# Index branch and S5 work moved between projection tiles, heads taken in pairs, and layer 0's S5 output table made by VectorE

## The reference

```python
for layer in range(DEPTH):                       # DEPTH = 2
    h = rms_norm(x, ln1_g[layer])
    (a_q, a_ckv, a_kr, i_q, i_k, i_w, b_u, c_q, c_kv, c_gate) = jnp.split(h @ w_in[layer], offsets, axis=-1)
    a_out = dsa_mixer(...)    # 4 heads; an indexer picks the 64 best keys of each query; latent keys and values
    b_out = s5_mixer(...)     # 16 groups of 16 channels, 64 complex states each, a linear scan over positions
    c_out = nsa_mixer(...)    # 8 heads, 2 key groups: compressed, selected and window branch, summed by gates
    mixed = jnp.concatenate([rms_norm(a_out, gain_a[layer]), rms_norm(b_out, gain_b[layer]),
                             rms_norm(c_out, gain_c[layer])], axis=-1)
    x = x + mixed @ w_out[layer]
    z = rms_norm(x, ln2_g[layer]) @ w_up[layer]  # 1024 -> 4096
    x = x + jnp.square(jax.nn.relu(z)) @ w_down[layer]
return rms_norm(x, final_g)
```

## Time and profile before

| what | us |
|---|---|
| median of 3 runs | 732.05 (731.47 to 738.36) |
| the profiled execution | 735.1 |
| its span, first to last instruction | 733.1 |
| TensorE clock granted, mean | 0.967 of full |

### The profile page before, as it was taken

The page is one execution under the profiler, slowest core; times in us unless marked ns, Lnnn a source line. Parts: engine busy times, 40 slices in busy tenths (PEclk is TensorE's granted clock), DMA queues, the critical chain, the costliest instruction groups (busy, mean ns, idle before and its releaser), DMA issues.

```text
span 733.1 us, 11482 instructions
## 1 busy us (share of the span) xinstructions
PE 664.8 (91%) x4308; PEld 586.9 (80%) x4308; DVE 450.8 (61%) x860; ACT 367.1 (50%) x680; POOL 228.2 (31%) x379
## 2 busy tenths in 40 slices
PE   5959878779899999999999987977989999999996
PEld 4847767568798899988978886756879889999884
DVE  8675974843755559596555659584375555455553
ACT  5542755563544543445545567556354444444542
POOL 5899433441034399980000001544100000000001
PEclk9988998998999999999999999999899999999998
DMA  9485020200685555637535722020065665666541
GB/s 267 125 220 149 30 41 30 73 30 29 202 237 201 170 186 169 225 119 247 168 119 164 228 79 41 30 73 30 29 202 178 196 188 171 208 182 198 177 140 57
DMA packets 62965, 102.77 MB, mean 140 GB/s; under 512 B 20677, under 2 KB 27022, under 8 KB 62878
## 3 DMA queue, kind: packets, MB, share of 16 engines
q1 hardware_dynamic: 58862, 98.63, 44.1%
q0 software_dynamic: 592, 1.70, 0.9%
q10 hardware_dynamic: 3456, 1.70, 0.9%
HBM read 99.66 MB, written 1.31 MB: 138 GB/s over the span
## 4 chain that ended last, share of the span: by engine, by line
PE 72%; DVE 14%; ACT 6%; issue 3%; DMA 2%; POOL 1%; SPq 0%; DVEq 0%; POOLq 0%; ACTq 0%
PE pb L1542 70%; DVE w_lo L1179 5%; DMA raw<-in_w_in 2%; DVE tab_zone L1437 2%; DVE x L1109 1%; ACT w_hi L804 1%; DVE dtmp L1102 1%; ACT tab_zone L1000 1%; PE pb L1675 1%; DVE h_lo L1109 1%; ACT ptmp L1007 1%; DVE cprob L1102 1%; PE pb L1825 1%; POOL sp L584 1%; ACT tab_zone L998 1%
## 5 line engine op out<-in xcount | busy, mean ns | idle before, releaser
L1179 DVE TENSOR_TENSOR w_lo<-raw,w_hi 128x1024 fp32r<-128x1024 f32 (+2 forms) x176 | 225.3, 1298 | 157.3 <-ACT w_hi L804 157.2
L804 ACT ACTIVATE w_hi<-raw 128x1024 fp32r<-128x1024 f32 (+2 forms) x184 | 187.7, 1026 | 224.4 <-PE pb L1542 200.4
L1542 PE MATMUL pb<-h_hi,w_hi 128*128 128x256 f32 x512 | 145.2, 284 | 2.5 <-DVE h_lo L1109 1.8
L1542 PE MATMUL pb<-h_hi,w_lo 128*128 128x256 f32 x512 | 144.9, 283 | 0.0
L1542 PE MATMUL pb<-h_lo,w_hi 128*128 128x256 f32 x512 | 144.9, 283 | 0.0
L1542 PEld LDWEIGHTS pb<-h_hi,w_hi 128*128 128x128 f32 x512 | 98.2, 192 | 4.1 <-DVE w_lo L1179 3.0
L1542 PE MATMUL pb<-w_hi,z_hi 128*128 128x512 f32 x256 | 99.9, 390 | 0.4 <-DVE w_lo L1179 0.4
L1542 PE MATMUL pb<-w_hi,z_lo 128*128 128x512 f32 x256 | 99.8, 390 | 0.0
L1542 PE MATMUL pb<-w_lo,z_hi 128*128 128x512 f32 x256 | 99.6, 389 | 0.0
L1542 PEld LDWEIGHTS pb<-h_hi,w_lo 128*128 128x128 f32 x512 | 98.2, 192 | 0.4
L1542 PE MATMUL pb<-w_hi,h_hi 128*128 128x512 f32 (+2 forms) x224 | 85.8, 383 | 13.9 <-DVE w_lo L1179 10.8
(11 more groups left out here) (304 smaller groups left out, 982.4 us busy)
## 6 DMA issues: line engine op xcount, KB each, us to landing
raw<-in_w_up SPq DMA_DIRECT2D x64, 512.0 KB, 3.7
raw<-in_w_down SPq DMA_DIRECT2D x64, 512.0 KB, 4.3
raw<-in_w_in SPq DMA_DIRECT2D x24, 512.0 KB, 4.7
raw<-in_w_out SPq DMA_DIRECT2D x16, 512.0 KB, 3.8
raw<-in_w_in SPq DMA_DIRECT2D x8, 308.0 KB, 3.5
raw<-in_w_in SPq DMA_DIRECT2D x8, 280.0 KB, 3.3
x<-in_x ACTq DMA_DIRECT2D x4, 256.0 KB, 4.2
u_zone<-proj SPq DMA_DIRECT2D x16, 32.0 KB, 2.1
```

Source lines behind the costliest of these rows:

```text
L804: hi_made.by(act.activation(w_hi[:, n % RING, 0:width(n)], raw[:, n % RING, 0:width(n)], ACT.Copy))
L1179: lo_made.by(dve.tensor_tensor(w_lo[:, n % RING, 0:width(n)], raw[:, n % RING, 0:width(n)], w_hi[:, n % RING, 0:width(n)].bitcast(F32), AL ...
L1542: return pe.matmul(o, l, r, start=start, stop=stop, skip_group_check=True)
```

## The change

It has four parts.

1. *Where branch work stands.* DVE's functions are named and put behind single low parts by a table `behind`; on PE `tile` takes a table of work to do after a quarter of a tile. The index heads are turned after tile 1, scored in the middle of tile 2 (four matmuls of 32 rows on four row groups), summed and half of the top-8 rounds done before the last tile ends. Queries, keys and latent rows are turned inside tile 4. In layer 1 the lag kernel stands before tile 1, and the row copies of S5's input and lags go through POOL's queue instead of SP's.
2. *Pairs.* 10 pairs replace 20 units. Head m of a pair sits on rows 64m to 64m+63 for scores and on columns 64m to 64m+63 for values, without padding. Scores of a pair fill banks 0 and 1, its transposes 2 and 3. The C heads' outputs change order, so gains and rows of `w_out` are loaded in that order (two transfers for such a piece). The first step of the output projection is done inside the loop (`out_first`).
3. *The table of layer 0.* The six operations of `ca` are made by DVE, one behind each of the low parts 8 to 12 and 14 (`far_re` ..), once POOL has made `pa` (`prep_a`); for layer 1 POOL makes it as before (`prep_far`).
4. *Setup.* No zeroing of `av` and `vpad`; sums and `r1` of layer 0 earlier; the table of Tanh and Exp loaded after piece 7 in layer 0.

```diff
+TWO_LOADS = (P_IN + 1, P_IN + 2, P_IN + 4, P_IN + 5)
...
-                        if n == 11:
+                        if L == 0 and n == 11:
                             sp.wait_ge(tile_sb.sem, tile_sb.at(L, 1))
...
+                            input_rows(sp, L)
...
+                if L:
+                    pool.wait_ge(tile_sb.sem, tile_sb.at(L, 1))
+                    input_rows(pool, L)
+                    pool.wait_ge(rk_sb.sem, rk_sb.at(L, 1))
+                    lag_rows(pool, L)
                 rstd(L, 2, rkv[:], stat[:, 2:4], A_RANK)
...
+                tt(pa[:, 0], pw[:, 0], pmag[:], ALU.mult, False)
+                prep_a.by(pool.tensor_tensor(pa[:, 1], pw[:, 1], pmag[:], ALU.mult))
...
+                def far_re():
+
+                    dve.wait_ge(prep_a.sem, prep_a.at(L, 1))
+                    dve.wait_ge(ct_sb.sem, ct_sb.at(L, 1))
+                    tt(ca[:, :, 0], A0, B0, ALU.mult)
...
+                if L == 0:
+                    behind = {8: (far_re,), 9: (far_re2,), 10: (far_re3,), 11: (far_im,), 12: (far_im2,), 13: (index_sum,),
+                              14: (far_im3, top), 15: (latent_heads,), 16: (top,), 17: (latent, top), 18: (queries,),
+                              19: (keys_s, second_weights, s5_lags, s5_sums_read, compressed_inputs)}
+                else:
+                    behind = {13: (index_sum,), 14: (top,), 15: (latent_heads, top), 16: (queries,), 17: (latent, top),
+                              19: (keys_s, second_weights, s5_sums_read, s5_states, s5_states_back, compressed_inputs)}
+                if L:
+                    s5_lags()
+                index_heads()
+                for n in range(8, 20):
+                    lo(n)
+                    for work in behind.get(n, ()):
+                        work()
+                D = int(L == 0)
+                between = {0: [keys_w, gates], 1: [c_open1], 2: [c_gelu], 3: [c_keys], 4: [c_max],
+                           5: [c_probs, top], 6: [top], 7: [top, a_mask], 8: [], 9: [], 10: [], 11: []}
...
+                if L:
+                    s5_kernel()
+                tile(1)
+                index_turned()
+                tile(2, {1: (index_scores,)})
+                u_transposed()
+                if L:
+                    s5_inputs()
+                    tile(3, {3: (s5_sums,)})
+                    tile(4, {0: (q_turned, latent_turned), 1: (kvc_turned, ks_turned)})
+                else:
+                    tile(3, {1: (s5_inputs,)})
+                    tile(4, {0: (q_turned, latent_turned), 1: (kvc_turned, ks_turned, s5_sums), 2: (s5_kernel,)})
...
+                between = {0: [a_rows, c_first, cq_first], 1: [kw_turned, aq_turned, ak_turned], 2: [cq_second],
+                           3: [c_second], 4: [c_scores], 5: [], 6: [c_transpose], 7: [], 8: [c_values], 9: [], 10: [], 12: [out_first]}
...
+                        for t, (a, n) in enumerate(((0, PART), (PART, SEQ))):
+                            for m in range(2):
+                                d = slice(HD * m, HD * m + HD)
+                                w = mm(pb[m][:, a:a + n], q[d, t * PART:(t + 1) * PART], k[d, 0:n], t == 0, True)
+                        s_ps.by(w)
...
+                        for t in range(TT):
+                            for m in range(2):
+                                w = mm(o[HD * m:HD * m + HD, t * PART:SEQ], vs[t][m],
+                                       pT[:, 2 * (v % 2) + m, t * SEQ:SEQ + t * PART],
+                                       t == 0 and v in (0, 2, C_PAIRS), t == 1 and last)
```

1027 lines of the change are left out of this document (567 added, 460 removed).

## The result

The changed kernel takes 699.97 us (median of 4 runs, 698.07 to 702.03) against 732.3 for the kernel before (4 runs beside it): a ratio of 0.9542, 95% interval 0.9484 to 0.96. The forecast was 694, with 676 to 714 as its range. The profiled execution has a span of 696.3 us where the sum gave 695.1.

A forecast was written before the change was run, and what follows sets the result against it. TensorE, busy 91% of the span, and its waits were taken as the bound. Layer 0 -17.5, layer 1 -18.5 and behind the loops -2.0 gave -38.0: span 695.1 from 733.1, 694 on the runs' scale, range 676 to 714.

The forecast's parts named there:

- Pairs of heads, PE's side: Loops: a pair costs PE 2.56 us instead of 3.84, as halves overlap; ten pairs save 12.8 us a layer.
- Layer 0's loop: First score to last value matmul in layer 0: 56 us, from 69.0, S5 states included.
- The mode's price: Loops: three tiling-mode changes a pair; sixty would cost 12 us if on the path, left to a rival.
- Layer 0's tiles: DVE makes the far table between low parts, taking turns with POOL; first score moves from 96.73 to 92.2.
- the work between pairs about 19 us in all ..., 34.5 us: Walk of DVE's list over ten pairs: top-8 steps, compressed branch and S5 output about 19, 34.5 us in all.
- Layer 1's loop: First score to last value matmul in layer 1: 56 us by 1.27 times PE's work; the walk gave 52.
- Layer 1's tiles: Tile 0 to first score in layer 1, branch work between tiles: first score at 439.4 instead of 447.77, 8.4 us.
- Behind the loops: An output piece of 2.7 us moves inside, a wait of about 1.7 is no longer covered: -1.0 a layer.
- Rival 1: Loops: packing buys little, row halves run in turn (13 us) or mode switches cost 12 us: 707, chance 0.20.
- Rival 2: Turn-taking in layer 0's tiles is milder, or the loop is closer to DVE's 34.5: 680, chance 0.16.
- Rival 3: Loops: single score buffers make a pair serial, 8.8 us one after another: 764, chance 0.06.
- rival 4: The move does nothing: holes return inside tiles, loops stay at 69 and 66: 719, chance 0.08.

The follow-up runs named there:

- e3: The changed kernel with each pair's four score matmuls issued twice in a row: 703.65 us, ratio 0.9582; the group of scores took 1.51 us.
- e5: The changed kernel with both heads' scores of a pair taken from the same half of the array: 707.68 us in one run; scores took 1.51 us.
- e1: The changed kernel with layer 0's far table moved back from DVE to POOL: 704.47 us, ratio 0.9602; first score at 93.30.
- e4: The changed kernel with the five top-8 steps between pairs of each layer's loop left out: 694.51 us, ratio 0.9466.
- e10: The changed kernel with layer 0's five top-8 steps and mask step moved out of the loop, behind low part 19: 697.83 us, ratio 0.9521.
- e7: The changed kernel with the S5 output turned one pair later in both layers, and layer 1's eight transfers ahead of output piece 24: 703.0 us, ratio 0.9563.
- e12: e11 with layer 0's S5 output turned one pair later, GLU and its split behind it: 696.1 us, ratio 0.9479.
- e11: e10 plus, in layer 1, two top-8 steps moved before low part 19 and the S5 output's transfers ahead of piece 24's loads: 696.75 us, ratio 0.9499.
- e8: The changed kernel with layer 0's far-table operations on DVE one low part later: 700.07 us, ratio 0.9527.

## Why the prediction was right, and where it was not

- **Pairs of heads, PE's side.** The 2.56 us a pair came out (2.46), but not by the sizes that it was made of: scores 0.86 for 0.64, values 0.80 for 0.64, transposes 0.80 for 1.28. The 1.28 had doubled a group of three that was read at a clock of 0.61; at full clock three take 0.33 and six would take 0.66. The price before was wrong by more: 3.28 for two units and not 3.84. So ten pairs save about 8.2 us of PE and not 12.8. That PE's busy time still fell to about the forecast's 44.4 is luck in part. Layer 0's loop lost 7.6 of 54.2 us where the sum had 9.8 off, and layer 1's, which started from 51.9, ended at 44.4 while the sum would have said 42.1. That halves of rows work side by side was assumed from halves of columns; e3 and e5 show it.
- **The mode's price.** The Trainium skill, "TensorEngine Tiling (Array Packing)", section Tiling Modes, says that a change of mode drains TensorE. The runs agree that it isn't free: 0.21 us in front of scores, which the row of before (0.20) had told, and by the sizes at full clock about 0.15 each in front of transposes (0.80 for 0.66) and values (0.80 for 0.65). The forecast had it at nothing. It is 0.5 us a pair, 10 over both layers, and the transposes sized too high hid it.
- **Layer 0's tiles.** Right in kind: DVE and POOL take turns from 35.6 on (forecast 36.9), DVE's big operations take 2.8 to 3.4 us each until 55, and the hole is cut up. First score at 90.50 for 92.2. e1 shows the table on DVE to be worth 2.8 us there; the 4.5 us of the medians are not clear of the noise. Missed: the gap of 8.22 us in DVE's list behind low part 19. "Then DVE reads lags and sums" was right; that it stood idle until then was there to be seen in the same walk.
- **Layer 0's loop.** Wrong: 56 forecast, 61.5 and 64.0 measured. The step that failed is "the work between pairs about 19 us in all ..., 34.5 us" of DVE: it was 44.45. Two things make up the 10 us. The S5 states, which now stand in this loop, take 5.7 us of DVE, and the 19 did not hold them. And collisions with POOL, which the prediction priced in the tiles, were left out in the loop: the mask's addition 2.59 for 0.63, the subtraction of the compressed maxima 1.93 for 0.42, a product of factors 1.69 for 0.17, each beside a low part of POOL (2.35 us alone). The kernel before had such collisions in its loops as well: a product of the pooled probabilities took 2.47 us at 137.51, beside a low part that ran from 137.33. With 6.5 us of DVE taken out (e4) or moved to the gap (e10) the loop comes to 58 to 60, part of it by the clock. Beside it stands the way back of the S5 output, 4.61 us of PE's waiting, which PE's timeline of the kernel before doesn't show in this loop, and which "PE for the pooled probabilities in pair 6" did not name. e7 and e12 took this wait away and the loop did not get shorter: 2.47 us of waiting for GLU's split came instead. What else separates 59 from 56 stays open.
- **Layer 1's loop.** 54.8 for 56: the ratio of 1.27 over PE's work was right here by size (54.8/44.7 = 1.23), and it says nothing of the cause. DVE's walk gave 52. Taking out top-8 steps alone did not shorten it (e4: 54.4, at a lower clock), nor did sending the transfers ahead with the turning a pair later (e7: 55.1). Both together, with the turning left in place, took 2.3 us off (e11, and again in e12). Which of the two matters was not separated further.
- **Layer 1's tiles.** 58.1 for 57.2. Each tile was as walked, within 0.4 us; the 0.9 us too much is about PE's wait of 1.10 for ACT inside the S5 tables. I tested no part of this term by itself: that the index branch and the turned blocks now lie between tiles is read from the trace, in which that 1.10 is PE's only wait between the start of tile 0 and its first scores (421.77).
- **Behind the loops.** -2.1 and -0.7 for -1.0 each. The piece of 2.7 us went inside; the wait that it used to cover was 0.35, not 1.7. Up to the first matmul of the MLP that gives -2.1 in both layers. In layer 1 the MLP then began at a granted clock of 0.50 (507.7 to 511.0, where the kernel before had 1.00), which took 1.4 us back.
- **Rivals.** Rival 1 fell in its first half: the halves do overlap. Its second half had the price of a switch right, but the time didn't come on top of the 2.56. Rival 2 fell: the first score came 1.7 us sooner than forecast and not 8, and the 34.5 that it leaned on was itself too low. Rival 3 fell, since pairs follow each other in 5.5 to 6.2 us; rival 4 fell with both loops.

So the good total is in part luck. Against the forecast changes, layer 0's loop missed 4.8 us and layer 1's tiles 0.9, the last stage 0.3; the first score, the stage behind loop 0 and layer 1's loop gave 1.7, 1.1 and 2.0 more than asked.

## What to carry to other kernels

Look at the granted clock of a stretch before taking a cost from it: a transpose group read at 0.61 was twice as dear as at 1.00, and the saving of a pair was overstated by half. Price a two-engine collision everywhere that the two engines meet: small DVE operations under POOL's low parts went from 0.2 to 0.6 us to 1.7 to 2.6. When a walk of an engine's list ends in "then it waits", the gap is a place to try for work that stands in a loop. And add up an engine's list from a window of the kernel before with what leaves and what comes, rather than from the items that come to mind: here 41.5 us, less 3.9 for three top-8 steps, plus 5.7 for the S5 states, is 43.3, where the walk had 34.5 and the trace 44.45.

## What the runs showed of the hardware

**The granted clock makes equal code unequal.** The S5 output matmuls of layer 0, in the changed kernel and in the second profile of the same kernel:

```profile
105.85 1.95 PE L1690 MATMUL pb<-ca,ez 128*32 128x128 f32 x64 [0.81 <-DVE ez L1345]
```

```profile
106.09 3.64 PE L1690 MATMUL pb<-ca,ez 128*32 128x128 f32 x64 [0.66 <-DVE ez L1345]
```

The granted clock of those stretches was 1.00 and 0.50 (2.4 and 1.2 GHz), after nearly equal PE waits of 2.30 and 2.19 us in front of the scores before. With no line changed, layer 0's loop was busy on PE for 46.7 us in one execution and 49.5 in the other, and took 61.5 and 64.0; layer 1's took 54.8 at a clock of 0.94 and 58.1 and 59.0 at 0.88 (e8, e1).

**Which DVE operations take turns with POOL.** Beside a low part on POOL, additions and products of two SBUF tensors waited (the mask 2.59, compressed maxima 1.93), and so did some operations with one SBUF input (a copy of 2.04 us for 0.29 beside POOL's input table). Score readings, which take one input from PSUM, kept their 0.28 and 0.42 us throughout; a reduction of `cprob` at 112.73 took its 0.42 beside a low part that ran from 112.47, and the top-8 step at 128.54 its usual time beside POOL's product. The Trainium skill, "SBUF — State Buffer", section "SBUF: two separate sides", has it so: a port pair that one of the two engines holds for a whole instruction, wanted by DVE operations in a 2-port mode or with two SBUF inputs. The trace agrees in size: 2.59 is near 0.56 plus the 2.17 that were left of POOL's low part when the addition began (130.84).

**Row halves.** Scores of two heads of 64 rows take 0.65 us for 768 columns side by side and 1.30 in one half, without the change of mode in front; the order of four such matmuls made no difference.
